# Two expert-mixture layers: all rows of an expert with over 64 rows go through wide blocks, and a wide block without rows loads no weights

## The chip, the cores and the metric

One core of a Trainium2 chip runs the whole program in one launch. The metric is the device time of one execution in microseconds (us), the median over several runs.

## The reference

Two transformer-like blocks work on 1024 tokens of width 1024, in fp32. Each ends in a mixture of 32 experts with two experts per token. This is the part that the change touches:

```
eid    = grp * EXPERTS_PER_GROUP + j_top          # two experts per token, 32 experts
counts = bincount(eid.reshape(-1), length=32)     # rows of each expert, 2048 in all
y_row  = (silu(x @ w_eg[e]) * (x @ w_eu[e])) @ w_ed[e]      # for each row of expert e
y      = segment_sum(y_row * gate, token)
```

w_eg and w_eu are 1024 x 512 for each expert, w_ed is 512 x 1024: 2.097 MB each, 6.29 MB for one expert. How many rows each expert gets follows from the inputs. Worked out by evaluating the reference on its own inputs, for experts 0 to 31:

```
first mixture   23  28  23   8  28  59  60  57   3  19  69  75 170  16  30  72
                28 115  79  20 118  40  45  55 239 193 104  52   4  29 114  73
second mixture  53  31  83  31  50  54  77  41  43  64  54  74  64  48  56  77
                50  28  42  73 131  60  63  73  93  40  89  70  97  72  87  80
```

## The kernel before, in words

`run_blocks` (L3866) does the first mixer, the first mixture (`moe_phase`, L40), the second mixer, and the second mixture (`mixed_moe`, L502). Each mixture has a router part, a loop (`expert_pairs`, L1118, the same code for both) and a part that combines the rows.

**The router part** computes the logits, picks two experts per token, counts the rows of each expert on DVE, and lays all rows out in blocks. There are wide blocks of 128 rows and small blocks of SB = 64 rows. One turn of the loop handles one wide block and one small block. For an expert with c rows the kernel before plans ceil((c - 64) / 128) wide blocks (none for up to 64 rows; expert 0 has at least one), and one small block if rows are left (L410 to L418 and L844 to L850; expert 1 always has a small block). With B wide and S small blocks the number of turns is `npair` = max(round up of (B + S) / 2, B) (L425 to L429). Small blocks beyond `npair` are put into the places of wide blocks behind the B wide ones. A column of `idx_w` holds, for each turn, the row index of the wide block's expert weights. Where the expert is the same as in the turn before, or the turn's number is `npair` or more, `again` (L492, L493) moves the index out of bounds, and the indirect DMA then moves nothing: the weights that lie in SBUF stay in use. A wide place without rows (when B + S is odd) gets expert 31 and its weights are loaded.

**The loop** runs `npair` turns. In a turn, TensorE does the wide block in three products (gate and up at L1244, L1245, L1249; down at L1271 to L1277) with the weights split into a high and a low part; ACT makes the high part (L1340) and DVE the low one (L1396). It does the small block in plain fp32 (up at L1259, down at L1287). A turn computes the same whatever rows it holds. Order on TensorE: wide gate and up, small gate and up, wide down, small down, transposes of the next rows. DVE scales the wide block's result (L1428, tile `m_yra`) and the small block's (L1432).

Three queues feed the loop. POOL gathers the rows (L1190) and loads the wide block's weights for the **next** turn, three indirect DMAs of 2 MB into `m_wa` (L1200), each as soon as DVE has read the old ones. SP loads the small block's weights, six plain DMAs of 1 MB into `m_wb` (L1172, L1175), each as soon as TensorE has used the old piece; the two pieces of w_ed (L1175) are issued at the end of a turn and used at the end of the next. This happens in every turn. ACT stores 0.75 MB of results per turn (L1367, L1370).

Of the kernel before, what the change touches and what calls it, by code (L numbers as in the profile page):

```python
# [6 lines left out]
P = 128  # L7
# [5 lines left out]
SB = 64  # L13
# [13 lines left out]
ALU = mybir.AluOpType  # L27
# [4 lines left out]
def bc(ap, n, axis):  # L32

    wide = ap.unsqueeze(axis)
    shape = list(wide.shape)
    shape[axis] = n
    return wide.broadcast_to(shape)


def moe_phase(nc, tag, x_in, mod, norm_w, w_rg, b_rg, w_re, b_re, w_gate, w_up, w_down, yrows, pool_dma, keep):  # L40
# [6 lines left out]
    NE, NG = w_gate.shape[0], w_re.shape[0]  # L47
# [6 lines left out]
    with ExitStack() as ctx:  # L54
# [12 lines left out]
        NB = NPAIR + 2  # L67
# [16 lines left out]
        with ExitStack() as c2:  # L84
            def sb2(name, shape, dt=F32):
                return c2.enter_context(nc.sbuf_tensor(f"{tag}_{name}", shape, dt))
# [20 lines left out]
            iota_s = sb2("iota_s", [P, NHI])  # L107
# [19 lines left out]
            M = sb2("M", [P, T, NE])  # L127
            Tc = sb2("Tc", [P, T, NE])
            cnt = sb2("cnt", [P, NE])
            cntb = sb2("cntb", [P, NE])  # L130
            nbig, nsml = sb2("nbig", [P, NE]), sb2("nsml", [P, NE])
            thr = sb2("thr", [P, NE])
            onese = sb2("onese", [P, NE])
# [3 lines left out]
            half, npair, over, gain = (sb2(n, [P, 1]) for n in ("half", "npair", "over", "gain"))  # L137
# [5 lines left out]
            later = sb2("later", [P, 1])  # L143
            isbig, upper = sb2("isbig", [P, 1]), sb2("upper", [P, 1])
            spread, weight, again = (sb2(n, [P, NB]) for n in ("spread", "weight", "again"))
            idf = sb2("idf", [P, 4])
            ids = sb2("ids", [P, 4], I32)
            ps_t = ps2("ps_t", [P, 2, J, P])
# [31 lines left out]
            with nc.Block() as block:  # L180
# [150 lines left out]
                def _(v):  # L331
                    n = [0]

                    def link(ins):
                        n[0] += 1
                        ins.then_inc(s_d, 1)
                        v.wait_ge(s_d, n[0])
# [3 lines left out]
                                                        op0=ALU.add, op1=ALU.mult))  # L341
# [3 lines left out]
                    for t in range(T):  # L345
# [11 lines left out]
                        if t >= RXS:  # L357
# [3 lines left out]
                                                       in1=srow[:, :], op0=ALU.mult, op1=ALU.mult).then_inc(s_xm, 1)  # L361
# [26 lines left out]
                    for t in range(T):  # L388
# [12 lines left out]
                                                        op0=ALU.add, op1=ALU.mult))  # L401
# [5 lines left out]
                    for t in range(1, T):  # L407
                        link(nc.vector.tensor_tensor(Tc[:, t, :], Tc[:, t - 1, :], ps_c[:, t - 1, :], ALU.add))
                    link(nc.vector.tensor_tensor(cnt[:, :], Tc[:, T - 1, :], ps_c[:, T - 1, :], ALU.add))
                    nc.vector.tensor_scalar(cntb[:, 0:1], cnt[:, 0:1], float(SB), None, ALU.add)  # L410
                    link(nc.vector.tensor_copy(cntb[:, 1:NE], cnt[:, 1:NE]))
                    link(nc.vector.tensor_scalar(nbig[:, :], cntb[:, :], 1.0 / P, (P - 1.0 - SB) / P - 0.5 + 0.5 / P, ALU.mult, ALU.add))
                    link(nc.vector.tensor_scalar(nbig[:, :], nbig[:, :], ROUND, None, ALU.add))
                    link(nc.vector.tensor_scalar(nbig[:, :], nbig[:, :], -ROUND, None, ALU.add))
                    link(nc.vector.tensor_scalar(nbig[:, 0:1], nbig[:, 0:1], 1.0, None, ALU.max))
                    link(nc.vector.tensor_scalar(thr[:, :], nbig[:, :], float(P), None, ALU.mult))
                    link(nc.vector.tensor_tensor(nsml[:, :], cnt[:, :], thr[:, :], ALU.is_gt))
                    link(nc.vector.memset(nsml[:, 1:2], 1.0))  # L418
                    for n_, end, st in ((nbig, bend, bst), (nsml, send, sst)):
                        link(nc.vector.tensor_tensor_scan(end[:, :], onese[:, :], n_[:, :], 0.0, ALU.mult, ALU.add))  # L420
                        link(nc.vector.tensor_tensor(st[:, :], end[:, :], n_[:, :], ALU.subtract))
                    n_big, n_sml = bend[:, NE - 1:NE], send[:, NE - 1:NE]
# [14 lines left out]
                                                        op0=ALU.mult, op1=ALU.add))  # L437
# [9 lines left out]
                                                        in1=bc(bbase[:, :], T, 1), op0=ALU.mult, op1=ALU.add))  # L447
# [5 lines left out]
                    for Mk, pos in ((M1, pos1), (M2, pos2)):  # L453
# [8 lines left out]
                                                            op0=ALU.mult, op1=ALU.add))  # L462
# [22 lines left out]
                                                        op0=ALU.mult, op1=ALU.add))  # L485
# [4 lines left out]
                    v.wait_ge(s_we, 1)  # L490
                    link(nc.vector.tensor_scalar(weight[:, :], ps_e, float(P), iota_p[:, 0:1], ALU.mult, ALU.add))
                    link(nc.vector.tensor_tensor(again[:, 1:NB], weight[:, 1:NB], weight[:, 0:NB - 1], ALU.is_equal))  # L492
                    link(nc.vector.scalar_tensor_tensor(out=again[:, 1:NB], in0=iota_s[:, 1:NB], scalar=npair[:, 0:1],  # L493
                                                        in1=again[:, 1:NB], op0=ALU.is_ge, op1=ALU.add))
                    link(nc.vector.scalar_tensor_tensor(out=idx_w[:, 1:NB], in0=again[:, 1:NB], scalar=8.0 * NE * P,
                                                        in1=weight[:, 1:NB], op0=ALU.mult, op1=ALU.add))
# [5 lines left out]
def mixed_moe(nc, tag, mix, mod, norm_w, w_rg, b_rg, w_re, b_re, w_gate, w_up, w_down, final_w, x_out, yrows, pool_dma):  # L502
# [6 lines left out]
    NE, NG = w_gate.shape[0], w_re.shape[0]  # L509
# [6 lines left out]
    with ExitStack() as ctx:  # L516
# [8 lines left out]
        NB = NPAIR + 2  # L525
# [22 lines left out]
        with ExitStack() as c2:  # L548
            size = [4 * (D + D // 2 + 12 * WF)]

            def sb2(name, shape, dt=F32):
                size[0] += 4 * math.prod(shape[1:])
                return c2.enter_context(nc.sbuf_tensor(f"{tag}_{name}", shape, dt))

            def ps2(name, shape, dt=F32):
# [7 lines left out]
            nbig, nsml, thr, bend, send, bst, sst, sbase, bbase, early = (  # L563
                sb2(n, [P, NE]) for n in ("nbig", "nsml", "thr", "bend", "send", "bst", "sst", "sbase", "bbase", "early"))
            half, npair, over, gain, later, isbig, upper = (
                sb2(n, [P, 1]) for n in ("half", "npair", "over", "gain", "later", "isbig", "upper"))
            spread, weight, again = (sb2(n, [P, NB]) for n in ("spread", "weight", "again"))
            idf, ids = sb2("idf", [P, 4]), sb2("ids", [P, 4], I32)
            if mixed_bytes > size[0]:
                sb2("pad", [P, (mixed_bytes - size[0]) // 4])  # L570
# [9 lines left out]
            tokf, iota_s = sb2("tokf", [P, T]), sb2("iota_s", [P, NHI])  # L580
            nb0, onese = sb2("nb0", [P, NE]), sb2("onese", [P, NE])
# [8 lines left out]
            ps_n, ps_r = acc[:, 0, 0:NE], acc[:, 0, 512:512 + T * NE].rearrange("p (t e) -> p t e", e=NE)  # L590
# [14 lines left out]
            with nc.Block() as block:  # L605
# [160 lines left out]
                def _(v):  # L766
                    n = [0]

                    def link(ins):
                        n[0] += 1  # L770
                        ins.then_inc(s_d, 1)
                        v.wait_ge(s_d, n[0])
# [43 lines left out]
                    mix_low(v)  # L816
                    nc.vector.memset(L[:, :, NG:8], NEG)
                    nc.vector.memset(onese[:, :], 1.0)
                    nc.vector.memset(nb0[:, 1:NE], (P - 1.0 - SB) / P - 0.5 + 0.5 / P)
                    nc.vector.memset(nb0[:, 0:1], (P - 1.0) / P - 0.5 + 0.5 / P)  # L820
                    link(nc.vector.memset(Mc[:, 0, :], 0.0))
                    for t in range(shares[0]):
                        mix_evict(v, t)
# [2 lines left out]
                                                        op0=ALU.add, op1=ALU.mult))  # L826
# [17 lines left out]
                    link(nc.vector.scalar_tensor_tensor(out=nbig[:, :], in0=ps_n, scalar=1.0 / P, in1=nb0[:, :], op0=ALU.mult, op1=ALU.add))  # L844
                    link(nc.vector.tensor_scalar(nbig[:, :], nbig[:, :], ROUND, None, ALU.add))
                    link(nc.vector.tensor_scalar(nbig[:, :], nbig[:, :], -ROUND, None, ALU.add))
                    link(nc.vector.tensor_scalar(nbig[:, 0:1], nbig[:, 0:1], 1.0, None, ALU.max))
                    link(nc.vector.tensor_scalar(thr[:, :], nbig[:, :], float(P), None, ALU.mult))
                    link(nc.vector.tensor_tensor(nsml[:, :], ps_n, thr[:, :], ALU.is_gt))
                    link(nc.vector.memset(nsml[:, 1:2], 1.0))  # L850
                    for n_, end, st in ((nbig, bend, bst), (nsml, send, sst)):
                        link(nc.vector.tensor_tensor_scan(end[:, :], onese[:, :], n_[:, :], 0.0, ALU.mult, ALU.add))
                        link(nc.vector.tensor_tensor(st[:, :], end[:, :], n_[:, :], ALU.subtract))
                    n_big, n_sml = bend[:, NE - 1:NE], send[:, NE - 1:NE]
# [14 lines left out]
                                                        op0=ALU.mult, op1=ALU.add))  # L869
# [9 lines left out]
                                                        in1=bc(bbase[:, :], T, 1), op0=ALU.mult, op1=ALU.add))  # L879
# [5 lines left out]
                    for Mk, pos in ((M1, pos1), (M2, pos2)):  # L885
# [8 lines left out]
                                                            op0=ALU.mult, op1=ALU.add))  # L894
# [8 lines left out]
                                                        op0=ALU.add, op1=ALU.mult))  # L903
# [19 lines left out]
                                                        op0=ALU.mult, op1=ALU.add))  # L923
# [4 lines left out]
                    v.wait_ge(s_we, 1)  # L928
                    link(nc.vector.tensor_scalar(weight[:, :], ps_e, float(P), iota_p[:, 0:1], ALU.mult, ALU.add))
                    link(nc.vector.tensor_tensor(again[:, 1:NB], weight[:, 1:NB], weight[:, 0:NB - 1], ALU.is_equal))  # L930
                    link(nc.vector.scalar_tensor_tensor(out=again[:, 1:NB], in0=iota_s[:, 1:NB], scalar=npair[:, 0:1],
                                                        in1=again[:, 1:NB], op0=ALU.is_ge, op1=ALU.add))
                    link(nc.vector.scalar_tensor_tensor(out=idx_w[:, 1:NB], in0=again[:, 1:NB], scalar=8.0 * NE * P,
                                                        in1=weight[:, 1:NB], op0=ALU.mult, op1=ALU.add))
# [2975 lines left out]
```

## Time and profile before

| | us |
|---|---|
| median of 3 runs (2985.73 to 2987.93) | 2985.74 |
| the profiled execution | 2986.39 |
| its span, first to last instruction | 2984.6 |
| first loop, about | 1018 to 1590 |
| second loop, about | 2377 to 2935 |

The span has 39013 instructions; the mean granted TensorE clock is 0.941 of full speed. What lies around the span (launch and end) is 1.8 us. The two loops are 38% of the span.

### The profile page before, as it was taken

Reading aid. Unit: us, or ns where it says so; the run is one execution under the profiler, and the core shown is the slowest. Engines: PE = TensorE matmul, PEld = TensorE weight load, DVE = VectorE, ACT = ScalarE, POOL = GpSimd, SP = SyncE. Lnnn points to the kernel's source line nnn. Section 1 sums busy time; section 2 is a strip of 40 time slices with the busy share of each in tenths; the row PEclk is TensorE's granted clock in tenths of the full one; section 3 lists DMA queues with packets and bytes.
Section 4 is the critical chain, followed back from the end, with each engine's and each line's share of the span. In section 5 each row is a group of like instructions: output and inputs, shape, how many; then the busy total and the mean of one; then the engine's idle time right before and its main releaser. Section 6 shows DMA issues by size and latency. Waiting matters only on the chain. (4 is left out here: it accounts for less than half of the span.)

```text
span 2984.6 us, 39013 instructions
## 1 busy us (share of the span) xinstructions
PE 2659.2 (89%) x14546; PEld 2003.0 (67%) x14546; DVE 1818.7 (61%) x2245; ACT 1089.5 (37%) x1295; POOL 461.6 (15%) x468
## 2 busy tenths in 40 slices
PE   4999995988798799999997898899779799999998
PEld 2888784765477666667664686788658666666664
DVE  3766365896634666666666755573445766666665
ACT  4323222653312244445444421233221154444443
POOL 0000000000000132223223121111000122232232
PEclk6999997999899899999998999899889899999999
DMA  6652374687733699999996315443652599999996
GB/s 242 246 180 75 112 270 148 206 266 281 279 128 152 271 423 425 424 363 362 426 424 228 95 57 109 77 121 107 237 209 85 212 395 425 420 422 421 418 416 232
DMA packets 277633, 775.07 MB, mean 260 GB/s; under 512 B 39079, under 2 KB 161507, under 8 KB 231704
## 3 DMA queue, kind: packets, MB, share of 16 engines
q1 hardware_dynamic: 219248, 473.87, 43.8%
q0 software_dynamic: 29168, 241.21, 19.7%
q10 hardware_dynamic: 29112, 58.54, 5.4%
q8 instruction: 71, 1.16, 0.2%
q14 instruction: 34, 0.28, 0.0%
HBM read 698.39 MB, written 113.67 MB: 272 GB/s over the span
## 5 line engine op out<-in xcount | busy, mean ns | idle before, releaser
L1396 DVE TENSOR_TENSOR m_ringl<-m_wa,m_ringh 128x2048 fp32r<-128x2048 f32 x214 | 489.3, 2287 | 142.8 <-ACT m_ringh L1340 141.8
L1340 ACT ACTIVATE m_ringh<-m_wa 128x2048 fp32r<-128x2048 f32 x214 | 409.6, 1915 | 287.2 <-PE m_ps_y L1277 184.1
L1259 PE MATMUL m_ps_b<-m_wb,m_xTb 128*64 128x256 f32 x2240 | 251.9, 382 | 7.4 <-DMA m_wb<-in_w_dram 6.8
L1851 PE MATMUL xp_acc<-xp_xh,xp_wh 128*128 128x512 f32 (+3 forms) x600 | 223.5, 373 | 6.5 <-DVE xp_xl L2134 6.5
L1259 PEld LDWEIGHTS m_ps_b<-m_wb,m_xTb 128*64 128x64 f32 x2240 | 157.6, 137 | 98.1 <-issue 13.5
L1852 PE MATMUL xp_acc<-xp_xl,xp_wh 128*128 128x512 f32 (+3 forms) x600 | 221.0, 368 | 0.0
L1853 PE MATMUL xp_acc<-xp_xh,xp_wl 128*128 128x512 f32 (+3 forms) x600 | 221.0, 368 | 0.0
L3030 PE MATMUL xq_acc<-xq_xh,xq_wh 128*128 128x512 f32 x448 | 181.3, 405 | 13.6 <-PEq L3099 6.4
L3032 PE MATMUL xq_acc<-xq_xh,xq_wl 128*128 128x512 f32 x448 | 178.6, 399 | 0.0
L3031 PE MATMUL xq_acc<-xq_xl,xq_wh 128*128 128x512 f32 x448 | 178.6, 399 | 0.0
L1287 PE MATMUL m_ps_b<-m_wb,m_hTb 128*64 128x512 f32 x560 | 142.2, 646 | 31.1 <-DMA m_wb<-in_w_dram 17.7
L3020 POOL TENSOR_TENSOR xq_wl<-xq_raw,xq_wh 128x1024 fp32r<-128x1024 f32 (+1 forms) x32 | 78.2, 2444 | 361.0 <-ACT xq_wh L3015 361.0
L1851 PEld LDWEIGHTS xp_acc<-xp_xh,xp_wh 128*128 128x128 f32 (+1 forms) x600 | 112.5, 187 | 28.9 <-issue 9.2
L1853 PEld LDWEIGHTS xp_acc<-xp_xh,xp_wl 128*128 128x128 f32 (+1 forms) x600 | 112.3, 187 | 20.4
L1852 PEld LDWEIGHTS xp_acc<-xp_xl,xp_wh 128*128 128x128 f32 (+1 forms) x600 | 112.6, 188 | 19.7
L1244 PE MATMUL m_ps_ga<-m_ringh,m_xTah 128*128 128x512 f32 x280 | 118.3, 422 | 2.4 <-issue 2.4
L1187 POOL COPY m_rowb<-m_idxb 128x1 int32 x35 | 69.4, 1983 | 322.5 <-PE m_ps_x L1234 322.5
L1271 PE MATMUL m_ps_y<-m_ringh,m_hTah 128*128 128x512 f32 x280 | 116.4, 416 | 0.0
L2024 DVE TENSOR_TENSOR xp_wl<-xp_raw,xp_wh 128x1024 fp32r<-128x1024 f32 (+1 forms) x29 | 34.7, 1197 | 132.0 <-ACT xp_wh L1933 132.0
L1245 PE MATMUL m_ps_ga<-m_ringh,m_xTal 128*128 128x512 f32 x280 | 113.9, 407 | 0.0
L1340 ACT ACT_TABLE_LOAD x35 | 44.9, 1283 | 185.8 <-issue 185.8
L1287 PEld LDWEIGHTS m_ps_b<-m_wb,m_hTb 128*64 128x64 f32 x560 | 37.6, 143 | 110.8 <-issue 68.4
(745 smaller groups left out, 5747.8 us busy)
## 6 DMA issues: line engine op xcount, KB each, us to landing
m_wb<-in_w_dram SPq DMA_DIRECT2D x102, 1024.0 KB, 24.5
m_wb<-in_w_eg_dram SPq DMA_DIRECT2D x36, 1024.0 KB, 18.9
m_wb<-in_w_eu_dram SPq DMA_DIRECT2D x36, 1024.0 KB, 26.0
m_wb<-in_w_ed_dram SPq DMA_DIRECT2D x36, 1024.0 KB, 23.3
yrows<-xp_steps SPq DMA_DIRECT2D x48, 512.0 KB, 6.8
mt_ring<-in_w_ada_dram SPq DMA_DIRECT2D x24, 1024.0 KB, 11.1
yrows<-m_yra ACTq DMA_DIRECT2D x35, 512.0 KB, 9.4
xp_mring<-in_w_mod_dram SPq DMA_DIRECT2D x32, 512.0 KB, 5.9
```

Of the source, the lines that this page charges most:

```text
L1244: nc.tensor.matmul(out[:, :], xT_ah[:, j, :], w_h[:, k, :], start=(j == 0), stop=False)
L1259: last = nc.tensor.matmul(ps_b[c * SB:(c + 1) * SB, p // 2, :], xT_b[:, k, h * SB:(h + 1) * SB], w[:, k, c * HF:(c + 1) * HF], start=(h == ...
L1271: nc.tensor.matmul(o, hT_ah[:, k, :], w_h[:, c, cols], start=(k == 0), stop=False)
L1287: last = nc.tensor.matmul(ps_b[d * SB:(d + 1) * SB, :, :], hT_b[:, c, h * SB:(h + 1) * SB], w[:, c, d * NF:(d + 1) * NF], start=(k == 0), ...
L1340: nc.scalar.activation(ring_h[:, h, :], w_a[p][:, h * WF:(h + 1) * WF], ACT.Copy).then_inc(s_wh, 1)
L1396: nc.vector.tensor_tensor(ring_l[:, h, :], w_a[p][:, h * WF:(h + 1) * WF], ring_h[:, h, :].bitcast(F32), ALU.subtract).then_inc(s_wl, 1)
L1851: nc.tensor.matmul(o, h, xh[:, j, a:a + w], start=(j == 0), stop=False)
L1852: nc.tensor.matmul(o, h, xl[:, j, a:a + w], start=False, stop=False)
L1853: last = nc.tensor.matmul(o, l, xh[:, j, a:a + w], start=False, stop=(j == J - 1))
L3030: nc.tensor.matmul(o, wh[:, n % 2, j, :], x_h[:, j, tok], start=(j == 0), stop=False)
L3031: nc.tensor.matmul(o, wh[:, n % 2, j, :], x_l[:, j, tok], start=False, stop=False)
L3032: last = nc.tensor.matmul(o, wl[:, n % 2, j, :], x_h[:, j, tok], start=False, stop=(j == k - 1))
```

## The change

In both router parts, an expert with over 64 rows gets ceil(c / 128) wide blocks and no small one; an expert with up to 64 rows gets a small block. In `again` the turns from `filled` = max(S + B - npair, B) on, instead of those from `npair` on, get an index out of bounds: `filled` is the number of wide places that hold rows. The loop is the same. The diff without its context (the two router parts are changed alike):

```
@@ moe_phase
-            cntb = sb2("cntb", [P, NE])
+            filled = sb2("filled", [P, 1])
-                    nc.vector.tensor_scalar(cntb[:, 0:1], cnt[:, 0:1], float(SB), None, ALU.add)
-                    link(nc.vector.tensor_copy(cntb[:, 1:NE], cnt[:, 1:NE]))
-                    link(nc.vector.tensor_scalar(nbig[:, :], cntb[:, :], 1.0 / P, (P - 1.0 - SB) / P - 0.5 + 0.5 / P, ALU.mult, ALU.add))
+                    link(nc.vector.tensor_scalar(nbig[:, :], cnt[:, :], 1.0 / P, (P - 1.0) / P - 0.5 + 0.5 / P, ALU.mult, ALU.add))
                     link(nc.vector.tensor_scalar(nbig[:, :], nbig[:, :], ROUND, None, ALU.add))
                     link(nc.vector.tensor_scalar(nbig[:, :], nbig[:, :], -ROUND, None, ALU.add))
+                    link(nc.vector.scalar_tensor_tensor(out=nbig[:, :], in0=cnt[:, :], scalar=SB + 0.5, in1=nbig[:, :],
+                                                        op0=ALU.is_gt, op1=ALU.mult))
...
-                    link(nc.vector.scalar_tensor_tensor(out=again[:, 1:NB], in0=iota_s[:, 1:NB], scalar=npair[:, 0:1],
+                    link(nc.vector.tensor_scalar(filled[:, :], n_sml, n_big, npair[:, 0:1], ALU.add, ALU.subtract))
+                    link(nc.vector.tensor_tensor(filled[:, :], filled[:, :], n_big, ALU.max))
+                    link(nc.vector.scalar_tensor_tensor(out=again[:, 1:NB], in0=iota_s[:, 1:NB], scalar=filled[:, 0:1],
                                                         in1=again[:, 1:NB], op0=ALU.is_ge, op1=ALU.add))
@@ mixed_moe: the same, and
-                    nc.vector.memset(nb0[:, 1:NE], (P - 1.0 - SB) / P - 0.5 + 0.5 / P)
-                    nc.vector.memset(nb0[:, 0:1], (P - 1.0) / P - 0.5 + 0.5 / P)
+                    nc.vector.memset(nb0[:, :], (P - 1.0) / P - 0.5 + 0.5 / P)
```

## Rows read from the trace of the kernel before

**Rows 1.** The page, busy time of an engine, share of the span, instructions:

```profile
PE 2659.2 (89%) x14546; PEld 2003.0 (67%) x14546; DVE 1818.7 (61%) x2245; ACT 1089.5 (37%) x1295; POOL 461.6 (15%) x468
```

**Rows 2.** The first loop, cut at the starts of the `m_yra` products (L1428):

```profile
core 0: us, PE busy (x) PEld busy (x) DVE busy (x) ACT busy (x) POOL busy (x), PEclk, DMA share, GB/s
1048.54:1139.73 91.19, 91.13 (x512) 63.16 (x510) 63.18 (x48) 44.84 (x31) 29.80 (x30) 1.00 1.01 423
1139.73:1175.94 36.21, 32.97 (x172) 22.09 (x170) 21.06 (x16) 14.93 (x11) 7.59 (x10) 0.91 1.01 425
1175.94:1206.39 30.45, 30.45 (x172) 20.88 (x170) 21.07 (x16) 14.93 (x11) 9.91 (x10) 1.00 1.01 423
1206.39:1241.73 35.34, 31.98 (x172) 21.31 (x170) 21.05 (x17) 14.95 (x11) 9.75 (x10) 0.95 1.01 424
1241.73:1272.93 31.20, 30.60 (x172) 20.96 (x170) 21.06 (x17) 14.94 (x11) 9.92 (x10) 1.00 1.01 424
1272.93:1309.16 36.23, 32.84 (x172) 21.98 (x170) 21.05 (x16) 14.90 (x11) 7.59 (x10) 0.91 0.91 366
1309.16:1339.53 30.37, 30.37 (x172) 21.06 (x170) 21.07 (x16) 14.94 (x11) 9.90 (x10) 1.00 0.87 345
1339.53:1491.37 151.84, 151.84 (x852) 105.17 (x850) 105.37 (x80) 74.70 (x51) 49.54 (x50) 1.00 0.97 394
1491.37:1527.63 36.26, 32.89 (x172) 21.99 (x170) 21.07 (x17) 14.93 (x11) 7.58 (x10) 0.91 1.01 426
1527.63:1588.40 60.77, 60.77 (x342) 42.12 (x340) 42.16 (x33) 29.91 (x21) 19.82 (x20) 1.00 0.83 346
```

**Rows 3.** The second loop, cut in the same way (columns as in rows 2):

```profile
2409.04:2500.63 91.59, 91.16 (x512) 63.07 (x510) 63.15 (x48) 44.84 (x31) 28.09 (x30) 1.00 1.01 423
2500.63:2535.33 34.70, 32.07 (x172) 21.56 (x170) 21.06 (x16) 14.91 (x11) 7.61 (x10) 0.95 1.01 424
2535.33:2571.83 36.50, 33.10 (x172) 22.17 (x170) 21.07 (x16) 14.91 (x11) 7.61 (x10) 0.91 1.00 418
2571.83:2602.37 30.54, 30.38 (x172) 21.01 (x170) 21.06 (x16) 14.95 (x11) 10.10 (x10) 1.00 1.01 422
2602.37:2635.55 33.18, 30.60 (x172) 20.96 (x170) 21.06 (x17) 14.95 (x11) 10.04 (x10) 1.00 1.01 425
2635.55:2736.24 100.69, 93.05 (x512) 63.49 (x510) 63.24 (x48) 44.80 (x31) 27.68 (x30) 0.98 1.01 421
2736.24:2899.62 163.38, 155.74 (x852) 106.04 (x850) 105.31 (x80) 74.69 (x51) 49.92 (x50) 0.98 1.00 417
2899.62:2931.57 31.95, 30.60 (x172) 20.95 (x170) 21.06 (x16) 14.94 (x11) 10.04 (x10) 1.00 0.60 245
```

**Rows 4.** The timeline of TensorE (start, duration, instruction), a stall of the first loop:

```profile
1139.53 1.94 PE L1287 MATMUL m_ps_b<-m_wb,m_hTb 128*64 128x512 f32 x8
1144.71 3.68 PE L1287 MATMUL m_ps_b<-m_wb,m_hTb 128*64 128x512 f32 x8 [3.24 <-DMA m_wb<-in_w_ed_dram]
```

**Rows 5.** The page, a DMA queue: packets, MB, share of 16 engines:

```profile
q0 software_dynamic: 29168, 241.21, 19.7%
```

**Rows 6.** The page, DMA issues: count, KB each, us to landing:

```profile
m_wb<-in_w_dram SPq DMA_DIRECT2D x102, 1024.0 KB, 24.5
yrows<-m_yra ACTq DMA_DIRECT2D x35, 512.0 KB, 9.4
```

**Rows 7.** The timeline, the end of the first router part and the loop's first product:

```profile
986.59 0.15 DVE L410 TENSOR_SCALAR m_cntb<-m_cnt 128x1 f32<-128x1 f32 x1
...
986.87 0.18 DVE L412 TENSOR_SCALAR m_nbig<-m_cntb 128x32 f32<-128x32 f32 x1
...
990.11 0.16 DVE L429 TENSOR_TENSOR m_npair<-m_half,m_bend 128x1 f32<-128x1 f32 x1
...
991.15 0.30 DVE L435 TENSOR_SCALAR m_sbase<-m_sbase,m_gain,m_over 128x32 f32<-128x32 f32 x1
...
1011.35 0.20 DVE L495 SCALAR_TENSOR_TENSOR m_idxw<-m_again,m_weight 128x33 int32<-128x33 f32 x1
...
1013.81 1.94 PE L1293 MATMUL m_ps_x<-m_ident,m_xa 128*128 128x128 f32 x8 [3.30 <-PEq L180]
```

More of the change, by code:

```diff
@@ L567, in mixed_moe @@
             spread, weight, again = (sb2(n, [P, NB]) for n in ("spread", "weight", "again"))
+            filled = sb2("filled", [P, 1])
             idf, ids = sb2("idf", [P, 4]), sb2("ids", [P, 4], I32)
@@ L846, in _ @@
                     link(nc.vector.tensor_scalar(nbig[:, :], nbig[:, :], -ROUND, None, ALU.add))
+                    link(nc.vector.scalar_tensor_tensor(out=nbig[:, :], in0=ps_n, scalar=SB + 0.5, in1=nbig[:, :],
+                                                        op0=ALU.is_gt, op1=ALU.mult))
                     link(nc.vector.tensor_scalar(nbig[:, 0:1], nbig[:, 0:1], 1.0, None, ALU.max))
@@ L930, in _ @@
                     link(nc.vector.tensor_tensor(again[:, 1:NB], weight[:, 1:NB], weight[:, 0:NB - 1], ALU.is_equal))
-                    link(nc.vector.scalar_tensor_tensor(out=again[:, 1:NB], in0=iota_s[:, 1:NB], scalar=npair[:, 0:1],
+                    link(nc.vector.tensor_scalar(filled[:, :], n_sml, n_big, npair[:, 0:1], ALU.add, ALU.subtract))
+                    link(nc.vector.tensor_tensor(filled[:, :], filled[:, :], n_big, ALU.max))
+                    link(nc.vector.scalar_tensor_tensor(out=again[:, 1:NB], in0=iota_s[:, 1:NB], scalar=filled[:, 0:1],
                                                         in1=again[:, 1:NB], op0=ALU.is_ge, op1=ALU.add))
```

## The prediction

> **What bounds the kernel now.** The page comes first: TensorE has work in 89% of the span [rows 1], so I look for stretches in which it waits or runs slowly. The change touches only the two expert loops and the router code ahead of them, so I cut each loop into its turns. A turn here is the time from one start of the product at L1428 to the next; turn k ends with the product of block pair k, counted from 0. The reader should see two things in these windows. First, there is a floor of 30.37 us per turn, in which TensorE is busy for all 30.37 us (the window at 1309.16) [rows 2]. Second, some turns take 31 to 36.5 us [rows 2, 3], and nearly all of them have a DMA share of 1.01 and 420 to 426 GB/s. Both limits are close together. A turn with all its weights moves 12 pieces of 1 MB (12.58 MB), 0.79 MB of results (512 KB, and 2 x 128 KB of the small block) [rows 6] and its gathered rows (2048 rows of 4 KB are 8.39 MB, over 18 or 17 turns 0.47 or 0.49 MB): 13.84 and 13.86 MB. At 424 and 422 GB/s this is 32.6 and 32.85 us, 2.2 and 2.5 us more than the floor. Measured over turns 1 to 8 of the first loop: 1309.16 - 1048.54 = 260.6 us, 32.6 per turn. So DMA is the bound by 2 us, and TensorE stands right behind it.
>
> How the lateness shows: three turns pass at the floor, then TensorE waits for the second piece of the small block's w_ed, 3.24 us, and does the next eight products in 3.68 us where the eight before took 1.94 [rows 4]. In this turn the granted clock is 0.91, a mix of the two levels, 1.2 and 2.4 GHz; it fell after the wait. The turn is 5.84 us over the floor. Turns 6 and 8 have the like (4.97, 5.86) [rows 2].
>
> Turns without wide weights exist already. By the counts of the reference, the first loop has B = 15, S = 20, 18 turns, and experts 24 and 25 have two wide blocks each, in turns 8, 9 and 10, 11. So turns 9 and 11 load nothing: 16 loads. The second has B = 15, S = 18, 17 turns, 17 loads. That the chip routes like this is seen in the software queue: 33 x 6.29 = 207.6 MB, plus gathers in the loops (2 x 8.39) and behind them (2 x 8.39), give 241.2 MB, and the queue has 241.21 [rows 5]. What a skipped load does stands in rows 2: in turns 8 and 9, where turn 9's and turn 10's transfers run, the DMA share falls to 0.91 and 0.87; turns 9 to 14 all take the floor (30.37 and 151.84 for five), and the fourth turn behind the last skipped one, turn 15, stalls again, by 5.89.
>
> **What the change does.** Expert 12 (170 rows) now has 2 + 0 blocks instead of 1 + 1, and so has expert 20 (131 rows) of the second mixture. B and S become 16 and 19, and 16 and 17; the sums stay 35 and 33, hence the turns 18 and 17. No turn goes away. Second blocks stand in turns 4, 10, 12 of the first loop and 7 of the second, and both sums are odd, so the last turns, 17 and 16, load nothing either. Loads: 14 and 15, four fewer, 25.2 MB. At 424 GB/s each is worth 14.8 us of DMA time. What of it comes out as time is decided turn by turn.
>
> *First loop, us over the floor.* Now: turns 1 to 3 0.08, then 5.84, 0.08, 4.97, 0.83, 5.86, then 0 to turn 14, 5.89, and 0.03 for the last two: 23.6. After: the transfers for turn 4 are left out while turn 3 runs, so the small block's w_ed comes early and turn 4 doesn't stall; turns 5 to 7 are free, turn 8 is the fourth and stalls by 5.86, turn 9 has 0.08 (as 5 now), 10 to 15 are free, 16 is the fourth behind 12 and stalls by 5.89; turn 17 was free already, so its left-out load buys nothing. Sum 11.9, a gain of **11.6**.
>
> *Second loop.* Now: 0.48 for turns 1 to 3, then 4.33, 6.13, 0.17, 2.81, 9.58 (8 to 10), 11.53 (11 to 15), 1.58: 36.6 [rows 3]. After: turns 1 to 6 as now, 11.1; turn 7 0.1; then the count of three begins anew, 0.4 for 8 to 10, and turns 11 to 15 do what 4 to 8 do now (with 3.67 for turn 8): 17.1. The left-out load of turn 16 takes its 1.58 away, 0.1 stays. Sum 28.8, a gain of **7.8**. Another reading of turns 11 to 15 has what they cost now, 11.5, since the queue can't be later there than it is now: a gain of 13.4. I take the first, because both loops cost the same 17.6 over eight full turns from a fresh start, and keep the second for the range.
>
> *Router code, per mixture.* L410 and L411 go in the first: 986.59 to 986.87, 0.28 us. The selection by `is_gt` is one linked instruction on 128x32; bounds are 0.16 (L429, on one column) and 0.30 (L435, with two scalars), each with a short gap behind it [rows 7]; it is nearest to L412, 0.18 on the same 128x32, so with its gap 0.25 at most. In the second only a memset off the path goes. Both lie on the path, -0.03 and +0.25. The two `filled` steps cost 0.4 to 0.7 together; they run between 1011 and the loop's first product at 1013.81 [rows 7], beside the store of the block table that the same barrier awaits. If that covers them they cost nothing, if not all. Together 0.2 to 1.7; I take **0.6**. Nothing else is issued: a skipped load keeps its POOL instructions, and the floor of turn 9 holds them.
>
> *Sum:* 11.6 + 7.8 - 0.6 = 18.8 us off the profiled execution's 2986.39, which is 2967.6. The median stands 0.65 below that execution, so 2967.
>
> **A rule weighed.** The rows show 420 to 426 GB/s in the full turns [rows 2, 3]. The Trainium skill, "DMA: Bandwidth & Descriptors", section "Where 436 GB/s comes from", says that for transfers between HBM and SBUF the HBM side binds, at about 358 GB/s per core. By that figure a turn would need 38.7 us, and no turn that follows a full turn could take 30.37; the trace disagrees, so the sum uses 424. By the rule each load left out would be worth 17.6 us, and four of them 70.
>
> **The rivals.**
> *B, every byte counts.* If DMA alone sets the loop, all four loads come out whole: 4 x 14.8 = 59, giving 2927. For it: share 1.01 in the full turns. Against it: share 0.87 in turn 9, which means that the queue runs dry, and the last turn, which has no lateness to take away. A half-way case is likelier: the stall at turn 16 fades (its neighbour, turn 17, loads nothing; 5.9 more), and the second loop gains 13 to 18: 30 to 35 in all, 2952 to 2957.
>
> *C, given back.* After a skip the stalls regroup. Each time TensorE waits for w_ed it loses clock besides; if the first loop keeps one stall more than forecast (a gain of 5.8), and the second gains only the 1.6 at its end and 0 to 3 of the middle, that is 7.4 to 10.4, less 0.2 to 1.7 for the router: 2976 to 2981. For it: the stalls of rows 3 come in no even beat. The skill's "TensorE: Matmul & The Clock Gate", section "HAM oscillation", says that repeated DMA waits make the clock fall again each time; the 0.91 and 0.95 of the stalled turns agree, the 1.00 of the turn at 2602, 2.81 over the floor, does not.
>
> *D, slower: one more turn.* If B alone passed 18, or B + S passed 36 (34 in the second), the loop would run another turn, 30.4 us: 2967 + 30 = 2997. The price is the floor; the point is the count of blocks. Against it: the rows in q0 match the counts, and the change trades a small block for a wide one. It needs counts that the queue's bytes speak against.
>
> *E, it does less than it says.* If the last turn's place still got an index in bounds, only two loads would go; the gain falls by 1.6, still inside the forecast.
>
> **How the numbers follow.** About 0.2% (6 us) is what a measurement of this kernel can tell from no change. Forecast, 2958 to 2975: 0.60. Half-way between it and B, 2945 to 2958: 0.20. B whole: 0.03. C: 0.14, of which a third to a half lies within 0.2% (above 2979.8). D and other losses: 0.03. Range: 2950 to 2978. Faster 0.88, same 0.08, slower 0.04.
>
> **What would show it.** q0 with 216.0 MB; 18 and 17 turns; a floor of still 30.37 us; first loop: no stall in turn 4, one at 8, none at 15, one at 16; second: turns 7 to 10 at the floor and stalls from 11 on; the first product of each loop at most 1 us later after its counts. I am wrong if turns cost more than the floor right behind a skipped load, if the floor moves, if the number of turns changes, or if what the loops save doesn't arrive at the end.

## The result, and the profile after

The changed kernel takes 2970.91 us, the median of 5 runs (2969.38 to 2974.46), against 2985.74 (5 runs, 2982.05 to 2987.93). The ratio is 0.9946 with a 95% interval of 0.9932 to 0.9959, a gain of 16 us (12 to 20); the two medians lie 14.8 us apart. The forecast was 2967 in a range of 2950 to 2978. A second set on another chip gave a ratio of 0.9956 (0.9941 to 0.9970). The profiled execution has a span of 2969.1 us, 15.5 less than before.

The software queue (the queue of the indirect DMAs) first: it says how many loads went away. The page of the changed kernel, DMA queue (compare [rows 5]):

```profile
q0 software_dynamic: 29168, 216.05, 17.8%
```

241.21 - 216.05 = 25.2 MB, four loads of 6.29 MB, as planned. Then the first loop, cut at the starts of the `m_yra` products, as in [rows 2]:

```profile
core 0: us, PE busy (x) PEld busy (x) DVE busy (x) ACT busy (x) POOL busy (x), PEclk, DMA share, GB/s
1049.45:1140.63 91.18, 91.13 (x512) 63.22 (x510) 63.18 (x49) 44.82 (x31) 29.78 (x30) 1.00 1.01 419
1140.63:1171.00 30.37, 30.37 (x172) 21.08 (x170) 21.07 (x16) 14.93 (x11) 9.89 (x10) 1.00 0.88 342
1171.00:1231.79 60.79, 60.73 (x342) 42.13 (x340) 42.15 (x32) 29.88 (x21) 19.88 (x20) 1.00 1.01 423
1231.79:1268.16 36.37, 32.19 (x172) 21.55 (x170) 21.07 (x16) 14.94 (x11) 9.90 (x10) 0.95 1.01 425
1268.16:1299.62 31.46, 30.58 (x172) 20.97 (x170) 21.05 (x16) 14.94 (x11) 9.90 (x10) 1.00 1.02 424
1299.62:1481.80 182.18, 182.18 (x1022) 126.43 (x1020) 126.39 (x96) 89.62 (x61) 59.38 (x60) 1.00 0.95 384
1481.80:1513.73 31.93, 30.60 (x172) 20.90 (x170) 21.07 (x16) 14.93 (x11) 9.90 (x10) 1.00 1.01 425
1513.73:1548.94 35.21, 31.85 (x172) 21.77 (x170) 21.07 (x16) 14.90 (x11) 7.58 (x10) 0.95 0.90 369
1548.94:1579.30 30.36, 30.36 (x172) 21.07 (x170) 21.08 (x17) 14.95 (x11) 9.90 (x10) 1.00 0.27 95
```

Turn 4, the row at 1140.63, is where the left-out load stands: 30.37 us instead of 36.21, and its DMA share falls to 0.88. Turns 5 and 6 run at the floor, turns 7 and 8 pay 6.00 and 1.09 us over it, turns 9 to 14 nothing, 15 and 16 pay 1.56 and 4.84. In the last row the share is 0.27; in the same turn of the kernel before it was 0.65, in a turn of 30.40 us. The load for the empty place is gone, and TensorE takes as long as with it. The second loop:

```profile
2403.49:2495.02 91.53, 91.11 (x512) 63.13 (x510) 63.12 (x48) 44.81 (x31) 28.07 (x30) 1.00 1.01 423
2495.02:2529.10 34.08, 31.89 (x172) 21.48 (x170) 21.06 (x17) 14.92 (x11) 9.65 (x10) 0.95 1.01 425
2529.10:2565.66 36.56, 32.07 (x172) 21.63 (x170) 21.06 (x16) 14.94 (x11) 10.03 (x10) 0.95 1.01 426
2565.66:2597.39 31.73, 30.61 (x172) 20.98 (x170) 21.08 (x17) 14.95 (x11) 10.03 (x10) 1.00 0.89 358
2597.39:2688.79 91.40, 91.13 (x512) 63.20 (x510) 63.20 (x48) 44.81 (x31) 30.09 (x30) 1.00 0.96 395
2688.79:2721.03 32.24, 30.60 (x172) 21.00 (x170) 21.06 (x17) 14.94 (x11) 10.04 (x10) 1.00 1.01 426
2721.03:2757.30 36.27, 32.87 (x172) 22.02 (x170) 21.07 (x16) 14.90 (x11) 7.62 (x10) 0.91 1.01 424
...
2855.82:2916.77 60.95, 60.77 (x342) 42.13 (x340) 42.13 (x33) 29.88 (x21) 20.06 (x20) 1.00 0.62 239
```

Turns 7 to 9 run at the floor (91.40), and the four turns 7 to 10 take 123.64 us where they took 133.87 [rows 3]. The stalls come back at turns 10 and 11. Where the time went, in us:

| stretch | before | changed | difference | second profile of the changed kernel |
|---|---|---|---|---|
| ahead of the first loop's first product `m_yra` | 1048.54 | 1049.45 | +0.9 | 1052.12 |
| first loop, 17 turns (over 17 x 30.37) | 539.83 (23.5) | 529.85 (13.6) | -10.0 | 530.60 (14.3) |
| between the loops | 820.67 | 824.19 | +3.5 | 823.74 |
| second loop, 16 turns (over 16 x 30.37) | 522.53 (36.6) | 513.28 (27.4) | -9.3 | 513.66 (27.7) |
| behind it | 53.03 | 52.33 | -0.7 | 53.08 |

The loops give 19.2 us; 3.7 of them don't arrive in this span. Not all of the 19.2 is waiting: over the first loop TensorE's busy time falls from 525.79 to 519.98 us, over the second from 496.69 to 494.19, for the same number of products. So 8.3 us come from products that spent less time at the lower clock behind a wait, and 10.9 from the waits.

How far does a loop's sum repeat? Two later kernels change only the second mixture, so their first loop is the one of the kernel before, and it took 20.0 and 24.8 us over 17 x 30.37, against 23.5 here. Sums of single profiles are good to some 2 us either way, and the stalls don't keep to their turns: turns 4 and 5 of that loop lost 5.84 and 0.08 us here, 3.32 and 6.04 in one of the two. With the new blocks three profiles of the first loop have 13.6, 13.7 and 14.3.

### The profile page after: what moved, and what is told of

Read it like the earlier page. It is cut to its first block and busy times, and to the rows that moved or that the text cites. A ratio compares the mean times of both kernels' runs of the same rounds, so it can differ in the third digit from the quotient of the medians.

```text
span 2969.1 us, 39016 instructions
## 1 busy us (share of the span) xinstructions
PE 2656.2 (89%) x14546; PEld 2008.4 (68%) x14546; DVE 1819.7 (61%) x2248; ACT 1089.5 (37%) x1295; POOL 471.6 (16%) x468
## 3 DMA queue, kind: packets, MB, share of 16 engines
q0 software_dynamic: 29168, 216.05, 17.8%
q8 instruction: 71, 1.16, 0.2%
## 5 line engine op out<-in xcount | busy, mean ns | idle before, releaser
L1265 PE MATMUL m_ps_b<-m_wb,m_xTb 128*64 128x256 f32 x2240 | 254.6, 386 | 14.3 <-DMA m_wb<-in_w_dram 10.1
L1265 PEld LDWEIGHTS m_ps_b<-m_wb,m_xTb 128*64 128x64 f32 x2240 | 159.0, 138 | 105.9 <-issue 15.5
L3036 PE MATMUL xq_acc<-xq_xh,xq_wh 128*128 128x512 f32 x448 | 182.3, 407 | 13.6 <-PEq L3105 6.4
L1293 PE MATMUL m_ps_b<-m_wb,m_hTb 128*64 128x512 f32 x560 | 133.1, 614 | 13.1 <-DMA m_wb<-in_w_dram 7.5
L1250 PE MATMUL m_ps_ua<-m_ringh,m_xTah 128*128 128x512 f32 x280 | 111.0, 396 | 0.0
L1251 PE MATMUL m_ps_ua<-m_ringh,m_xTal 128*128 128x512 f32 x280 | 111.0, 396 | 0.0
## 6 DMA issues: line engine op xcount, KB each, us to landing
m_wb<-in_w_eg_dram SPq DMA_DIRECT2D x36, 1024.0 KB, 14.8
```

The lines of the kernel that those rows point to most:

```text
L1250: nc.tensor.matmul(out[:, :], xT_ah[:, j, :], w_h[:, k, :], start=(j == 0), stop=False)
L1251: nc.tensor.matmul(out[:, :], xT_al[:, j, :], w_h[:, k, :], start=False, stop=False)
L1265: last = nc.tensor.matmul(ps_b[c * SB:(c + 1) * SB, p // 2, :], xT_b[:, k, h * SB:(h + 1) * SB], w[:, k, c * HF:(c + 1) * HF], start=(h == ...
L1293: last = nc.tensor.matmul(ps_b[d * SB:(d + 1) * SB, :, :], hT_b[:, c, h * SB:(h + 1) * SB], w[:, c, d * NF:(d + 1) * NF], start=(k == 0), ...
L3036: nc.tensor.matmul(o, wh[:, n % 2, j, :], x_h[:, j, tok], start=(j == 0), stop=False)
```

## The experiments

Two theories stood against each other. **T**: a left-out load is worth the lateness that it finds, at most, because the queues can't run further ahead than the buffers. **R**: DMA is the bound, and each load is worth its 14.8 us wherever it stands. Nine runs were made; their edits are shown in short form. "Over the floor" always means the loop less 17 or 16 times 30.37 us. Each table of windows has the columns shown above.

### One half of the change: the blocks without `filled`

```diff
-    tensor_scalar(filled, n_sml, n_big, npair, ALU.add, ALU.subtract)
-    tensor_tensor(filled, filled, n_big, ALU.max)
-    ... again: iota_s >= filled
+    ... again: iota_s >= npair
```

> The change without `filled`: experts over 64 rows get only wide blocks, the last turns' empty wide places load expert 31 as before. Theory T (what a left-out load is worth depends on how late the weights are just then): first loop like the changed kernel's, 13.6 us over the floor of 30.37 us per turn; second loop like it up to turn 15 and 1.6 us more in turn 16; the whole within 2 us of the changed kernel, ratio to before about 0.995 to 0.996. Rival R (every byte counts, 14.8 us per left-out load): half of the changed kernel's gain, 29.6 of 59 us by its own price, so the ratio stands half-way between the changed kernel's and 1. Rival N (some of the difference outside the loops, 4.5 us, is caused by the change): the stretches ahead of the first loop and between the loops are as long as in the changed kernel (1049.5 and 824.2 us); if they vary by chance they differ from run to run.

Measured: 2972.07 us, ratio 0.9942 (0.9924 to 0.9960), 222.34 MB in the software queue. The loops, and the stretch between them:

```profile
1049.41:1579.44 530.03, 519.82 (x2892) 359.07 (x2890) 358.00 (x273) 254.00 (x171) 163.95 (x170) 0.99 0.96 394
1579.44:2403.43 823.99, 711.15 (x3559) 577.32 (x3557) 466.98 (x888) 240.02 (x322) 111.51 (x80) 0.92 0.46 142
2403.43:2917.48 514.05, 493.95 (x2722) 339.13 (x2720) 336.98 (x256) 238.97 (x161) 153.51 (x160) 0.98 0.95 392
```

13.7 and 28.1 us over the floor, against 13.6 and 27.4 (14.3 and 27.7 the second time) with all of the change. The queue has three loads fewer than before, not two as expected: in the new order of the second loop the empty last place, expert 31, stands right behind a block of expert 31, so `again` leaves its load out by itself. Only the first loop's last load came back, and it costs nothing that shows: the point estimates have this kernel 1 us above the changed kernel by the medians and no worse by the ratios. The gain belongs to the new blocks. The expectation gave R half of the gain, for two loads of four (a ratio of 0.9973, outside the interval). With three of four left out R would keep three quarters, a ratio of 0.9960, which stands at the interval's edge. So the times don't refute R here; the first loop does, which has its last load back, 14.8 us of DMA time, and took 0.2 us more. R by its own price, 3 x 14.8 = 44 us, is far outside.

### The other half alone

```diff
 (kernel before)
+    filled = max(n_sml + n_big - npair, n_big)
-    again: iota_s >= npair
+    again: iota_s >= filled
```

> The kernel before with only `filled`: 2 loads fewer, those of the last turns. T: the first loop gains nothing (23.5 over the floor), the second loop gains the 1.6 us of turn 16; ratio 0.9990 to 1.0003. R: 2 x 14.8 us, ratio 0.990.

Measured: 2986.60 us, ratio 0.9993 (0.9981 to 1.0004), 228.63 MB: two loads fewer. The profiled execution is the slowest of its twelve, 2995.62 us, so its loops may read a little long.

```profile
1051.15:1590.72 539.57, 523.05 (x2892) 359.76 (x2890) 358.00 (x272) 253.97 (x171) 161.76 (x170) 0.99 0.94 387
...
2416.00:2940.58 524.58, 496.46 (x2722) 338.71 (x2720) 336.89 (x256) 238.98 (x161) 155.55 (x160) 0.98 0.95 396
```

23.3 and 38.7 us over the floor. 12.6 MB less and nothing gained; even the 1.6 us that T allowed the second loop did not come (its last turn took 30.46 us, but the stalls ahead of it were 3.5 us longer, in one profile). R's 0.990 is far outside.

### The floor: no wide loads at all

```diff
-    again: (iota_s >= npair) + equal
+    again: (iota_s >= 0.5) + equal
```

> No wide block loads weights after turn 0 (the wide blocks compute with expert 0's weights; all else as before). T: every turn at 30.37 us, both loops under 1 us over the floor, so 59 us less in the loops: the most that any leaving-out of loads can bring. Rival (TensorE or DVE waits for something else too): turns remain above 31 us, or a floor that falls below 30.37 because DMA traffic slows the engines.

This kernel leaves out every wide load behind turn 0, so all wide blocks compute with expert 0's weights and the results are wrong. Measured, one execution: 2959.46 us.

```profile
1046.34:1562.72 516.38, 516.24 (x2892) 357.96 (x2890) 358.05 (x272) 254.07 (x171) 168.66 (x170) 1.00 0.65 240
...
2386.45:2904.69 518.24, 516.44 (x2892) 357.72 (x2890) 357.90 (x273) 254.07 (x171) 168.76 (x170) 1.00 0.64 239
```

The first loop is 0.1 us over the floor with a DMA share of 0.65. So the floor of 30.37 us isn't set by the weight traffic, and TensorE is busy for 516.24 us of it. The second loop had 18 turns here, since the first mixture's other results change the routing; 518.24 / 17 = 30.48 us per turn, the floor again. With that extra turn the whole time can't be compared with the others; the loops can.

### Every fourth turn

```diff
 (kernel before, both mixtures)
+    for c in (4, 8, 12, 16): memset(again[:, c:c+1], 1.0)
```

> The kernel before, with the wide loads of turns 4, 8, 12, 16 left out in both loops (those turns compute with the weights of the turn before). 8 loads fewer than before, of 33. T (three free turns behind each left-out load): no stall anywhere, both loops under 2 us over the floor, as if no load were left. T with the shorter fuse that the changed kernel shows (a stall in the third turn, at the small block's up weights): some of turns 3, 7, 11, 15 stall by up to 6 us each, 20 us in all. R: 8 x 14.8 us is more than the whole excess of 60, so the floor too. What tells T from R is the number per load: R has no stall in any third turn.

Turns 4, 8, 12 and 16 compute with the weights of the turn before. Measured, one execution: 2928.85 us, 190.89 MB.

```profile
1049.41:1565.75 516.34, 516.28 (x2892) 357.98 (x2890) 357.97 (x272) 253.97 (x171) 168.38 (x170) 1.00 0.91 368
...
2386.28:2873.96 487.68, 486.02 (x2722) 336.74 (x2720) 336.86 (x256) 239.07 (x161) 158.55 (x160) 1.00 0.94 387
```

0.1 and 1.8 us over the floor: not one stall in 33 turns, though three of four turns still load 12.6 MB. Eight left-out loads do what all 31 do. Spread like this, a left-out load is worth 58 / 8 = 7.3 us. The total doesn't tell T from R, for R too has more than the whole excess to give. None of the third turns (3, 7, 11, 15) stalled either, where T with a shorter fuse allowed 20 us. In these turns the transfers for the next one are missing, which would explain it: the changed kernel's turn 7, a third turn with the next turn's transfers in it, does stall.

### A load left out too early, and two in a row

Both kernels change only the second mixture of the kernel before, so that the first loop and the routing stay. The turns named compute with the weights of the turn before.

```diff
+    memset(again[:, 1:2], 1.0)                       # the first kernel
+    memset(again[:, 7:8], 1.0); memset(again[:, 8:9], 1.0)   # the second
```

> The kernel before; in the second loop turn 1 loads no wide weights (it computes with turn 0's). One load fewer, as in the change's turn 7, but at a place where nothing is late yet. T: the count of three free turns starts one turn later, so the stalls of the second loop move by one turn and only the last of them drops out: 33 to 36 us over the floor (36.6 to 38.7 in the kernels with the old order). R: 14.8 us less, 22 to 24. The first loop as before, 23 to 24.

> The kernel before; in the second loop turns 7 and 8 load no wide weights. T: the first of the two takes away the lateness (about 9 us in the loop, as in the change), the queue then runs dry, and the second adds only one turn's deficit of 2.5 us and what stands at the end of the beat: 23 to 26 us over the floor, against 27.4 to 28.1 with turn 7 alone. R: 14.8 us less than with one, about 13.

Measured, one execution each: 2990.53 and 2977.76 us. The second loop with turn 1 left out:

```profile
2415.27:2537.34 122.07, 121.52 (x682) 84.21 (x680) 84.19 (x65) 59.74 (x41) 38.16 (x40) 1.00 0.99 407
2537.34:2936.39 399.05, 375.02 (x2042) 255.23 (x2040) 252.80 (x193) 179.22 (x121) 113.12 (x120) 0.97 0.97 404
```

Four turns at the floor instead of three, then twelve with 399.05 - 12 x 30.37 = 34.6 us over it: 35.2 in all. A load of 14.8 us left out where nothing is late saves 1.4 us against [rows 3], less than two profiles of the old order differ by (36.6 and 38.7). With turns 7 and 8 left out the second loop took 509.20 us, 23.3 over the floor. One load at turn 7 (in the kernels with the new blocks, which leave out turn 16's too) gave 8.5 to 9.3 us, the second beside it 4 to 5. T's numbers held in both (33 to 36, and 23 to 26); R's (22 to 24, and 13) in neither. The first loops, the same in both, took 24.8 and 20.0 us over the floor where 23 to 24 were expected.

### Less traffic from another side

```diff
-    act.dma_start(y_v[i][0:P], y_a[:, :])
+    act.dma_start(y_v[i][0:16], y_a[0:16, :])
-    act.dma_start(y_v[i][P:PAIR, ...], y_b[d * SB:(d + 1) * SB, :])
+    act.dma_start(y_v[i][P:P + 16, ...], y_b[d * SB:d * SB + 16, :])
```

> The kernel before, with 16 of the wide block's 128 rows and 16 of the small block's 64 rows stored per turn (the rest of the results is left out); all loads as before. 0.69 MB less per turn, so a turn asks for 13.15 MB, 31.1 us at 423 GB/s, 0.7 us over the floor instead of 2.2 to 2.5. T (the excess is the DMA deficit summed over the turns between left-out loads): a third of the excess or less, first loop under 8, second loop under 13 us over the floor (30.4 us more if the wrong rows change the second mixture's number of turns). Rival W (the weight queues alone set the pace, stores ride along): both loops as before, 23.5 and 36.6.

This kernel leaves out most of the result rows. Measured, one execution: 2946.86 us.

```profile
1050.75:1567.52 516.77, 513.65 (x2892) 359.98 (x2890) 358.14 (x272) 253.47 (x171) 160.73 (x170) 1.00 0.96 395
...
2390.75:2892.29 501.54, 488.83 (x2722) 338.48 (x2720) 336.93 (x257) 238.65 (x161) 152.73 (x160) 0.99 0.97 406
```

0.5 and 15.6 us over 30.37 per turn. All weight loads are there, and the first stall comes in turn 6 instead of turn 4. So the stores' bytes count with the others, and the rival in which the stores ride along falls. The first loop kept T's bound of 8, the second missed the one of 13. The free turns show a good part of why: they take 30.10 us here, so the floor itself fell by 0.27, and against the new floor the deficit is 31.1 - 30.1 = 1.0 us per turn, 16 over the loop; measured against that floor it is 501.54 - 16 x 30.10 = 19.9, and 5.1 in the first loop.

### The empty place in mid-loop

The last experiment follows from the others: the same four loads left out, but the one of the empty place moved to where the weights are late. The wide blocks of the experts from 20 on (first mixture) or 15 on (second) and the small blocks behind them move one turn down; the empty turn then has the expert of the turn before it, and `again` does the rest.

```diff
 (changed kernel)
-    over = n_big - npair
+    filled = max(n_sml + n_big - npair, n_big)
+    over = n_big - filled
+    gap = filled - npair                        # 0 or -1
+    bst[:, GAP:NE] -= gap                       # GAP = 20 or 15
...
+    turn = iota_p + (iota_p >= bend[GAP - 1]) * gap
-    early = bend <= iota_p;  later = iota_p + npair - n_big;  isbig = iota_p < n_big
+    early = bend <= turn;    later = turn + npair - n_big;    isbig = turn < n_big
-    again: iota_s >= filled
+    again: iota_s >= npair
```

> The changed kernel, but the wide place without rows stands in mid-loop instead of last: ahead of expert 20 in the first mixture (turn 8) and of expert 15 in the second (turn 4). Same 29 loads, same turns. T: first loop free but for the last four turns, about 6 us over the floor instead of 13.6; second loop: no stall before turn 12, then as eight full turns from a fresh start, 17.6 instead of 27.4; 2 x 1.2 us more router steps. Together 15 us under the changed kernel, ratio to before about 0.9895. R: the same bytes as the changed kernel, so the same time plus 2.4 us, ratio 0.995.

Measured: 2956.71 us, ratio 0.9909 (0.9894 to 0.9924), 216.05 MB, the same as the changed kernel. The two loops, each cut where its stalls begin:

```profile
1054.74:1510.37 455.63, 455.54 (x2552) 315.86 (x2550) 315.88 (x240) 224.12 (x151) 148.67 (x150) 1.00 0.97 395
1510.37:1576.67 66.30, 62.44 (x342) 42.41 (x340) 42.13 (x32) 29.84 (x21) 19.46 (x20) 0.97 0.81 336
2400.93:2705.89 304.96, 303.79 (x1702) 210.41 (x1700) 210.59 (x160) 149.42 (x101) 98.39 (x100) 1.00 0.98 405
2705.89:2902.74 196.85, 186.27 (x1022) 126.84 (x1020) 126.39 (x97) 89.62 (x61) 57.78 (x60) 0.98 0.95 396
```

Fifteen turns of the first loop at the floor (455.63 is 15 x 30.37 + 0.1), then 5.6 us in the last two; ten turns of the second at the floor (1.3 us over), then 14.6 in six. 5.6 and 15.9 us over the floor, where T said 6 and 17.6, and the changed kernel has 13.6 and 27.4: 19.4 us less in the loops with not one byte less. R's ratio of 0.995 lies outside the interval, T's 0.9895 inside. Not all of the 19.4 arrives: the stretch ahead of the first loop took 1054.74 us, with the longer router code, against 1049.45 and 1052.12 in the two profiles of the changed kernel. Against the kernel before it gains 27 us (23 to 32), against the changed kernel's 16. It beats both kernels. Its interval doesn't touch the changed kernel's, though the two were timed on different chips, each against the kernel before.

### The changed kernel again

> The changed kernel once more. If the pattern of the turns is set by the kernel, the first loop stalls again in turns 7, 8 and 15, 16 and nowhere else, 13 to 14 us over the floor, and the second costs 27 to 29. If what lies outside the loops varies by chance, the stretch ahead of the first loop and the one between the loops differ from the first profile's 1049.5 and 824.2 by 1 us or more, and ratio to before is 0.993 to 0.996 as the first time.

Measured: 2974.89 us, ratio 0.9956 (0.9941 to 0.9970). First loop 14.3 over the floor, with stalls in turns 7, 8, 15 and 16 and no others above 0.3 us; second 27.7. The turns that stall repeat. How a loss is shared between two neighbours doesn't: turns 7 and 8 lost 2.58 and 4.85 us, where it was 6.00 and 1.09. What lies ahead of the first loop doesn't either: 1052.12 instead of 1049.45.

## Why the prediction was right

**The bound.** Two limits 2 us apart, TensorE's 30.37 us and the queues' 32.6 to 32.85: shown, the first by the kernel without wide loads, the second by the short stores, which took the loops from 23.5 and 36.6 to 0.5 and 15.6 us over the floor. The second of these is 2.6 more than was allowed. The 30.37 us are not TensorE's products alone; see the last section.

**What is left out.** 216.0 MB, 18 and 17 turns, the floor of 30.37 us: all as forecast.

**The first loop**, forecast 11.6, measured 10.0 and 9.2. The stall forecast for turn 8 came in turn 7, at an earlier piece. The changed kernel's timeline of TensorE, beside [rows 4]:

```profile
1247.34 5.40 PE L1265 MATMUL m_ps_b<-m_wb,m_xTb 128*64 128x256 f32 x48
1256.92 3.54 PE L1265 MATMUL m_ps_b<-m_wb,m_xTb 128*64 128x256 f32 x16 [4.18 <-DMA m_wb<-in_w_eu_dram]
```

It is still turn 7's set of small weights that is late, but its fourth piece (up) and not its sixth (down). That holds for this one profile. In the second profile of the same kernel the down piece is waited for the longest, in turn 8, as forecast, behind a shorter wait in turn 7:

```profile
1257.77 1.95 PE L1265 MATMUL m_ps_b<-m_wb,m_xTb 128*64 128x256 f32 x16 [2.38 <-DMA m_wb<-in_w_eu_dram]
1272.52 2.53 PE L1293 MATMUL m_ps_b<-m_wb,m_hTb 128*64 128x512 f32 x8 [3.39 <-DMA m_wb<-in_w_ed_dram]
```

The kernel without `filled` does the like (1.56 and 3.38 us). So the fourth turn behind a left-out load pays most in two profiles of three, and the third turn pays 2.4 to 6.0 in all three, where the forecast had it free. Which piece is late changes from one execution to the next in the same loop. Turn 16 was forecast at 5.89 with turn 15 free; the two share 6.4 to 6.6 us in the three profiles.

**The second loop**, forecast 7.8, measured 9.3 and 8.9. Turns 10 and 11 stalled where 11 and 12 were forecast, turn 15 (3.67 forecast) did not stall, and the 1.58 of turn 16 is gone. But the last is no gain of `filled`: with the new blocks the load is left out without it too, and `filled` alone brings nothing. What a loop costs is a sum over its turns, and which turn shows it moves about.

**How much of it is luck.** The forecast for the loops was 19.4 us and 19.2 came, but the first loop's gain was 1.6 smaller than forecast and the second's 1.5 larger. The two cancel, and both are within what the same loop differs by from one execution to another (20.0 to 24.8 us over the floor). The mechanism and the size are borne out; agreement to 0.2 us is chance.

**The router code**, forecast 0.6 in all. First mixture: from the last count (L409) to the row index (L476) 20.63 us, 20.67 before. From the block table (L488) to the loop's first product, 4.35 against 4.32 before; the two `filled` steps lie between and are covered. The changed kernel:

```profile
1010.47 0.17 DVE L488 CAST m_ids<-m_idf 128x4 int32<-128x4 f32 x1
...
1012.04 0.27 DVE L493 TENSOR_SCALAR m_filled<-m_send,m_bend,m_npair 128x1 f32<-128x1 f32 x1
1012.35 0.16 DVE L494 TENSOR_TENSOR m_filled<-m_filled,m_bend 128x1 f32<-128x1 f32 x1
...
1014.82 1.52 PE L1299 MATMUL m_ps_x<-m_ident,m_xa 128*128 128x128 f32 x6 [3.33 <-PEq L180]
```

Second mixture: 0.2 us more ahead of the row index (20.08 against 19.86) and 0.2 behind the table. 0.4 in all.

**What the forecast lacked** is the 3.7 us outside the loops, one of its own signs of being wrong. Apart from the 0.6 us for the router code these stretches were taken as fixed, and they are not. Over ten profiles of this study, those of before and after among them, the stretch ahead of the first loop lies between 1046.3 and 1053.1 us, leaving out the last design with its longer router code, and the one between the loops between 820.5 and 825.3; kernels that change nothing there show nearly the whole spread (820.53 with every fourth load left out, 825.28 with `filled` alone). The profile before happened to be at the low end of the second. Whether the change adds a microsecond there stays open; the four profiles with the new blocks have 823.7 to 824.3.

**The rivals.** B, every byte counts: refuted, and with it the half-way case, as turn 16 still stalled and the second loop gained 9, not 13 to 18; the same 25.2 MB brought 19 us in the loops in one order and 39 in the other. C, given back: the stalls do regroup, but the sum holds. D, one more turn: 18 and 17 turns. E: the index of the empty place is out of bounds, and it doesn't matter.

**The rule weighed.** The full turns of the changed kernel move 419 to 426 GB/s, so the 358 GB/s at which, by the Trainium skill ("DMA: Bandwidth & Descriptors", "Where 436 GB/s comes from"), the HBM side binds is not the bound of this one core, before or after.

## What to carry to other kernels

Where two limits lie close together, a transfer that is left out is worth only the lateness that stands at that moment: 1.4 us or nothing at turn 1, nothing that shows in the last turn, 9 at turn 7, for the same 6.3 MB. So look for when the buffers run dry, not for how many bytes go, and put the light turns between the heavy ones: the same four left-out loads in a better order gave 11 us more.

Cut a loop into its turns before summing: the floor, the number of free turns behind a light one and the stall behind them were to be read in the kernel before to within some 2 us per loop. A second profile of the same kernel tells what in such a table is the kernel's and what is one execution's: by turn the stalls moved, by loop they stayed.

## What was not expected of the hardware

With the result stores cut to 16 rows, a free turn took 30.10 us instead of 30.37, while leaving out all wide weight loads (240 GB/s over the first loop instead of 398) didn't move it. The timelines show what hangs on the stores. The kernel before, in a turn that starts at 1339.53:

```profile
1343.99 1.16 ACTq L1370 DMA_DIRECT2D yrows<-m_yrb  x2
1348.80 2.29 DVE L1396 TENSOR_TENSOR m_ringl<-m_wa,m_ringh 128x2048 fp32r<-128x2048 f32 x1 [2.19 <-ACT m_ringh L1340]
1351.15 1.19 PE L1249 MATMUL m_ps_ua<-m_ringl,m_xTah 128*128 128x512 f32 x4
```

With short stores, in a turn that starts at 1296.52:

```profile
1300.96 0.80 ACTq L1370 DMA_DIRECT2D yrows<-m_yrb  x2
1305.44 2.29 DVE L1396 TENSOR_TENSOR m_ringl<-m_wa,m_ringh 128x2048 fp32r<-128x2048 f32 x1 [1.84 <-ACT m_ringh L1340]
1307.98 1.09 PE L1249 MATMUL m_ps_ua<-m_ringl,m_xTah 128*128 128x512 f32 x4
```

Issuing the small block's two stores holds ACT for 1.16 us, and for 0.80 with short ones. ACT's high part of the next weights, and behind it DVE's low part, start that much later: 9.27 us into the turn against 8.92. In the kernel before DVE ends at 1351.09 and TensorE's product with the low part starts at 1351.15, so it has waited for it. With short stores DVE ends at 1307.73 and the product starts at 1307.98, without a wait. That is 0.16 of the 0.27 us; the rest shows at the next group of products. The kernel without wide loads has the same 1.14 us of issue, and the same floor. So the floor holds a short wait behind ACT's store instructions, though TensorE is counted busy all through it. This is read from the timelines; no run changed the issue alone.
